# Eight modulation groups moved into the split weight stream, with the quarters of two projections between them

## The chip, the cores and the metric

The kernel runs on one core of a Trainium2 chip (trn2). TensorE (PE in the profile) does the matrix products, VectorE is DVE, ScalarE is ACT, GpSimd is POOL, and SyncE (SP) issues most of the transfers. The metric is the device time of one execution in microseconds; lower is better. The kernel before took 2410.05 us as the median of three runs (2409.24 to 2411.62).

## The reference, cut to what matters

Two transformer blocks work on 256 tokens of width 2048, all in float32. The change touches the start of the first block only: the modulation (a long vector times a 2048 x 12288 matrix, for two vectors `c` and `c_ctx`), the normalisation of `x` and `ctx`, and the first columns of the input projection.

```python
mod_l = (jax.nn.silu(c) @ w_ada[l] + b_ada[l])[:, None, :]
mod_c = (jax.nn.silu(c_ctx) @ w_ada[l] + b_ada[l])[None, None, :]
sh_a, sc_a, gt_a, sh_f, sc_f, gt_f = jnp.split(mod_l, 6, axis=-1)
csh_a, csc_a, cgt_a, csh_f, csc_f, cgt_f = jnp.split(mod_c, 6, axis=-1)
h_l = modulate(rms_norm(x, g_mix_norm[l]), sh_a, sc_a)      # h * (1 + scale) + shift
h_c = modulate(rms_norm(xc, g_mix_norm[l]), csh_a, csc_a)
qa_l, kva_l, kr_l, cb_l, cc_l, ch_l = split_projection(h_l @ w_in[l])
qa_c, kva_c, kr_c, cb_c, cc_c, ch_c = split_projection(h_c @ w_in[l])
```

Of the 24 groups of 512 columns of `w_ada`, groups 0 to 3 give the shift and 4 to 7 the scale that `h_l` and `h_c` need, so both vectors need groups 0 to 7; groups 8 to 23 are needed for `c` alone and later. The key-value columns of `w_in` (256 + 64) are applied to `h_l` and `h_c`, the query columns (512) to `h_l`.

## The kernel before, in words

**The weight stream.** All weights but `w_ada` come as chunks of 1 MB, 128 partitions x 2048 float32, in the order that `schedule()` (L63) writes down. SP loads chunk c into one of five buffers `raw` as soon as PE has finished chunk c-5 (L324 to L327). ACT copies a chunk into one of three buffers `hi`, rounded to fp32r (`split`, L379, L384), once PE has finished chunk c-3; DVE writes the remainder `lo` over `raw` (`split`, L921, L924). PE then makes three products for each pair of weight tile and activation tile: hi x hi, hi x lo, lo x hi (`three`, `chunk`). The activations have a hi and a lo part of the same kind (`act_hi`, `act_lo` for `x`, `u_hi`, `u_lo` for `ctx`). Every engine works through its own list in order and waits on semaphores.

**The modulation stream.** `w_ada` comes as 96 chunks of 1 MB of its own, four to a group, which POOL loads (L343). Groups 0 to 7 go through PE in plain float32, 2 columns (`silu_c` of both vectors) against 512 (`ada_rows`, L1900), into a row of PSUM; ACT copies the row out (L459) and PE turns it into columns (`ada_columns`, L1911). Four buffers serve here, two of which lie where `u_hi` and `u_lo` come later. Groups 8 to 23 are needed for one vector and are multiplied and summed on DVE, four instructions a chunk (`ada_chunk`, L931, L944), one chunk beside each chunk of the weight stream; PE only sums over the partitions (`ada_reduce`, L1855) and DVE adds the bias (`ada_take`).

**The order.** First come the modulation groups 0 to 7, with the normalisation of `x` and `ctx` beside them (L1088 to L1096). Then DVE applies scale and shift (`enter`, L1108) and makes the low halves in four quarters, and PE starts the key-value projection `kv_in` (4 chunks) and the query projection `q_in` (4 chunks). Modulation groups 8 and 9 run on DVE beside those two (`CARRY`, L313). Then comes a stretch of 46 chunks, counted by m: `conv_c0` (m 0 to 3), `kv_b` (4 and 5), `q_b` (6 to 9), `conv_in` (10 to 29) with the attention beside it, and `w_out` (30 to 45). At step m, ACT and DVE split the chunk m+2, and until m = 39 DVE takes one modulation chunk (L1301); PE reduces a group at m = 4, 8, ... 40 (L2040). Everything behind `w_out` is the same in both kernels.

## Time and profile before

| | |
|---|---|
| median of three runs | 2410.05 us |
| the profiled execution's own time | 2408.68 us |
| its span, first to last instruction | 2406.9 us |
| PE busy | 2319.2 us (96%), 17556 matmuls |
| DVE busy | 1505.5 us (63%) |
| ACT busy | 1008.8 us (42%) |
| moved by DMA | 471.85 MB, 196 GB/s on average |
| TensorE clock granted, mean | 0.986 of 2.4 GHz |

A busy PE is not a PE at its peak. The shares are means over the whole program; what one stage is worth is read from windows and from the chain of work that ended last. PEclk 1.00 stands for 2.4 GHz and 0.50 for 1.2 GHz.

### The profile page before, as it was taken

To read this page: it belongs to the slowest core of one execution; us is meant where nothing else is said; L and a number is where in the kernel's file an instruction comes from. 1 tells how busy PE (TensorE), PEld (TensorE's weight loads), DVE (VectorE), ACT (ScalarE), POOL (GpSimd) and SP (SyncE) were. 2 spreads that over 40 slices of the span, in tenths; PEclk is the share of its full clock that TensorE was granted. 3 is DMA by queue.
4 is the path that set the end of the run, shared out by engine and by line. 5 is a ranking of instruction groups with operands and counts; after the bars stand their busy time and mean duration, and the time that the engine had idled before them with its cause. 6 is when DMAs were issued, how large, how long until landed. Compare 5 with 4: busy or idle time off the path is not lost.

```text
span 2406.9 us, 39294 instructions
## 1 busy us (share of the span) xinstructions
PE 2319.2 (96%) x17556; PEld 2157.5 (90%) x17556; DVE 1505.5 (63%) x1703; ACT 1008.8 (42%) x965; POOL 59.0 (2%) x112
## 2 busy tenths in 40 slices
PE   6969989999999999999999899999999999999998
PEld 1249978898999999999999898989999999999998
DVE  2268787787888545555466758865567644445674
ACT  1023534433444334453344444445435435664352
POOL 1100000000000000000000000000000000000000
PEclk9989999999999999999999999999999999999999
DMA  9746765586676555555555454433544554334443
GB/s 394 277 146 258 295 232 212 213 309 247 243 265 246 201 181 182 186 178 190 177 190 191 155 181 158 154 112 138 178 174 160 190 182 156 118 140 175 168 162 126
DMA packets 64953, 471.85 MB, mean 196 GB/s; under 512 B 7216, under 2 KB 7216, under 8 KB 8336
## 3 DMA queue, kind: packets, MB, share of 16 engines
q1 hardware_dynamic: 50544, 365.65, 42.2%
q0 software_dynamic: 14096, 101.59, 11.2%
q8 instruction: 138, 2.26, 0.4%
q10 hardware_dynamic: 144, 2.10, 0.2%
q14 instruction: 31, 0.25, 0.0%
HBM read 467.21 MB, written 2.10 MB: 195 GB/s over the span
## 4 chain that ended last, share of the span: by engine, by line
PE 83%; DVE 10%; DMA 2%; ACT 2%; issue 2%; POOL 0%; DVEq 0%; ACTq 0%; POOLq 0%
PE acc L1780 72%; PE aux L1780 11%; DMA ada_raw<-ada_stream 2%; DVE lo L924 2%; ACT hi L384 1%; DVE ada_acc L944 1%; DVE x L1633 0%; DVE x L1630 0%; DVE rstd L1041 0%; DVE rstd L1057 0%; PE aux L1970 0%; DVE act_lo L1640 0%; ACT probs L727 0%; DVE rope_scratch L1479 0%; DVE rstd L1316 0%
## 5 line engine op out<-in xcount | busy, mean ns | idle before, releaser
L924 DVE TENSOR_TENSOR lo<-raw,hi 128x2048 fp32r<-128x2048 f32 x342 | 781.9, 2289 | 636.7 <-ACT hi L384 636.4
L384 ACT ACTIVATE hi<-raw 128x2048 fp32r<-128x2048 f32 x342 | 653.0, 1913 | 836.4 <-PE acc L1780 822.7
L1780 PE MATMUL acc<-act_hi,hi 128*128 128x256 f32 x4464 | 610.8, 289 | 36.5 <-DVE u_lo L1066 18.1
L1780 PEld LDWEIGHTS acc<-act_hi,hi 128*128 128x128 f32 x4464 | 570.6, 195 | 51.7 <-issue 40.4
L1780 PE MATMUL acc<-act_lo,hi 128*128 128x256 f32 x4464 | 591.8, 284 | 0.0
L1780 PE MATMUL acc<-act_hi,lo 128*128 128x256 f32 x4464 | 588.8, 283 | 0.0
L1780 PEld LDWEIGHTS acc<-act_lo,hi 128*128 128x128 f32 x4464 | 562.9, 193 | 0.0
L1780 PEld LDWEIGHTS acc<-act_hi,lo 128*128 128x128 f32 x4464 | 559.4, 192 | 0.0
L944 DVE SCALAR_TENSOR_TENSOR ada_acc<-ada_raw,silu_c,ada_acc 128x512 f32<-128x512 f32 x224 | 153.5, 743 | 6.8 <-DMA ada_raw<-ada_stream 6.2
L1780 PE MATMUL aux<-ada_raw,silu_c 128*2 128x512 f32 x256 | 113.6, 599 | 20.5 <-DMA ada_raw<-ada_stream 20.5
L1780 PEld LDWEIGHTS aux<-ada_raw,silu_c 128*2 128x2 f32 x256 | 20.8, 85 | 106.9 <-issue 94.1
L1780 PE MATMUL acc<-u_hi,hi 128*128 128x256 f32 x688 | 89.8, 283 | 0.0
L1780 PE MATMUL acc<-u_lo,hi 128*128 128x256 f32 x688 | 89.7, 283 | 0.0
L1780 PE MATMUL acc<-u_hi,lo 128*128 128x256 f32 x688 | 89.7, 283 | 0.0
L1780 PEld LDWEIGHTS acc<-u_lo,hi 128*128 128x128 f32 x688 | 85.7, 192 | 0.0
L1780 PEld LDWEIGHTS acc<-u_hi,lo 128*128 128x128 f32 x688 | 85.7, 192 | 0.0
L1780 PEld LDWEIGHTS acc<-u_hi,hi 128*128 128x128 f32 x688 | 85.7, 192 | 0.0
L636 ACT ACTIVATE y<-acc,vectors 128x256 f32<-128x256 f32 x86 | 41.7, 565 | 79.9 <-PE acc L1780 79.9
L343 POOL DMA_DIRECT2D ada_raw<-ada_stream x96 | 51.0, 532 | 701.8 <-DVE ada_acc L944 585.9
L1364 DVE SCALAR_TENSOR_TENSOR y<-acc,vectors,y 128x255 f32<-128x255 f32 x86 | 35.6, 475 | 49.3 <-ACT y L636 49.3
L727 ACT ACTIVATE probs<-probs,columns 128x256 f32<-128x256 f32 x32 | 16.0, 501 | 73.5 <-DVE columns L1568 73.5
L459 ACT ACTIVATE ada_acc<-aux 2x512 f32<-2x512 f32 x8 | 4.7, 585 | 98.9 <-PE aux L1780 98.9
(319 smaller groups left out, 1647.1 us busy)
## 6 DMA issues: line engine op xcount, KB each, us to landing
raw<-stream SPq DMA_DIRECT2D x342, 1024.0 KB, 4.8
ada_raw<-ada_stream POOLq DMA_DIRECT2D x96, 1024.0 KB, 5.4
x<-x_t SPq DMA_DIRECT2D x1, 2048.0 KB, 9.2
ctx<-ctx_t SPq DMA_DIRECT2D x1, 2048.0 KB, 16.1
x<-x_t ACTq DMA_DIRECT2D x1, 2048.0 KB, 8.9
out<-x SPq DMA_DIRECT2D x3, 512.0 KB, 7.5
p_raw<-p_t POOLq DMA_DIRECT2D x1, 512.0 KB, 4.8
out<-x SPq DMA_DIRECT2D x2, 256.0 KB, 2.0
```

Of the source, the lines that this page charges most:

```text
L343: eng.dma_start(ADA[slot][:, :], ada_stream[n]).then_inc(ada_full[slot], 16)
L384: nc.scalar.activation(HI[c % NH][:, :], RAW[c % NR][:, :], ACT.Copy).then_inc(hi_done, 1)
L459: nc.scalar.activation(FMA[ag % 2][0:2, 0, :], AUX[0:2, 1 + ag % 2, :], ACT.Copy)\
L636: nc.scalar.activation(Y[:, i, :], ACC[(base[0] + gi) % 2][:, t, :], ACT.Identity, scale=VV[:, bass.ds(w + 1, 1)], bias=VV[:, bass.ds(w + ...
L727: ins = nc.scalar.activation(s, s, ACT.Exp, bias=COL[:, 4 * (h % 2) + qt:4 * (h % 2) + qt + 1], accum_out=COL[:, 4 * (h % 2) + 2 + qt:4 * ...
L924: V.tensor_tensor(LO[c % NR][:, :], RAW[c % NR][:, :], HI[c % NH][:, :].bitcast(F32), ALU.subtract)\
L944: V.scalar_tensor_tensor(out=a, in0=w, scalar=s, in1=a, op0=ALU.mult, op1=ALU.add)\
L1364: ins = V.scalar_tensor_tensor(out=Y[:, i, 1:T], in0=acc[:, t, 0:T - 1], scalar=VV[:, bass.ds(w, 1)], in1=Y[:, i, 1:T], op0=ALU.mult, op1= ...
L1780: return TE.matmul(out, lhs, rhs, start=start, stop=stop, skip_group_check=True)
```

## The change

Groups 0 to 7 leave the modulation stream and enter the weight stream: each is four ordinary 1 MB chunks that ACT and DVE split into hi and lo. The stationary operand of PE is now four columns, the hi and lo part of both vectors (`C4`), and each of the four row blocks of a chunk takes one fp32r matmul with `hi` and one with `lo`, 8 a chunk. The 8 groups are ordered 0, 4, 1, 5, 2, 6, 3, 7, and one quarter of `kv_in` and of `q_in` (one chunk each) stands between them as soon as its quarter of shift and scale is known. Scale and shift are applied by ACT (`enter`), DVE keeps the low halves; the sums of squares are folded to four blocks by DVE additions and finished by PE (`tree`, `tree_total`) in place of a long DVE reduction. `x`, `consts` and `ctx` are loaded by the queue of ACT, ahead of its first work. Groups 8 and 9 move from beside `kv_in` and `q_in` into the stretch behind, so 48 modulation chunks stand in steps 4 to 41 by the list `ADA_STEPS` where 40 stood in steps 0 to 39; steps 4, 5, 10, 13, 15, 19, 21, 24, 29, 35 and 38 hold two. POOL loads the first two of them when PE has finished chunk 28.

```diff
+S0 = (("ada", 0), ("ada", 4), ("ada", 1), ("kv", 0), ("q", 0), ("ada", 5), ("ada", 2), ("kv", 1), ("q", 1), ("ada", 6),
+      ("ada", 3), ("ada", 7), ("kv", 2), ("q", 2), ("kv", 3), ("q", 3))
+ADA_ORDER = [i for kind, i in S0 if kind == "ada"]
+
+PLAN = [(kind, i, j) for kind, i in S0 for j in range(4 if kind == "ada" else 1)]
+ADA_END = [c for c, (kind, i, j) in enumerate(PLAN) if kind == "ada" and j == 3]
+
+ADA_STEPS = sorted([4, 4, 5, 5, 6, 7, 8, 9, 10, 10] + list(range(12, 42)) + [13, 15, 19, 21, 24, 29, 35, 38])
+BANK3_BUSY = (19, 21, 22, 23, 25, 26, 30, 31)
+REDUCE_AT, TAKE_AT = {}, {}
+for _g in range(12):
+    _m = ADA_STEPS[4 * _g + 3] + 1
+    while _m in BANK3_BUSY or _m in REDUCE_AT:
+        _m += 1
+    REDUCE_AT[_m] = 8 + _g
+    TAKE_AT[_m + 1] = 8 + _g
+
...
+    phases["kv_in"], phases["q_in"] = (0, 0), (0, 1)
+    for kind, i, j in PLAN:
+        if kind == "ada":
+            chunks.append(("w_ada", 0, list(range(4 * j, 4 * j + 4)), [(512 * i, 512 * i + 512)]))
+            continue
+        cols = [(Q_RANK, Q_RANK + KV_RANK), kr, kr] if kind == "kv" else [(0, Q_RANK)]
+        chunks.append(("w_in", 0, list(range(4 * i, 4 * i + 4)), cols))
+        if i == 3:
+            ENDS.append(("pe_chunk", len(chunks)))
+    groups[0] += 2
...
-            for n in range(4 * GTL):
-                if n >= 4:
-                    eng.wait_ge(ada_used, n - 3)
-                load(n, n % 4)
+            eng.wait_ge(pe_chunk, 28)
             for n in range(4 * GTL, 96):
-                if n < 4 * GTL + 2:
-                    eng.wait_ge(ada_used, n - 3)
-                else:
+                if n >= 4 * GTL + 2:
                     m = n - 2 - 4 * GTL
                     eng.wait_ge(ada_fma, 17 * (m // 4) + 4 * (m % 4 + 1))
                 load(n, n % 2)
...
-            def ada_row_copy(ag):
-                act.wait_ge(ada_used, 4 * ag + 4)
-                if ag >= 2:
-                    act.wait_ge(ada_sum, ag - 1)
-                nc.scalar.activation(FMA[ag % 2][0:2, 0, :], AUX[0:2, 1 + ag % 2, :], ACT.Copy)\
+            act.wait_ge(sem("silu_c"), 1)
+            nc.scalar.activation(C4[:, :, 0:2], SC[:, :].rearrange("p (v k) -> p k v", v=2), ACT.Copy)\
+                .then_inc(sem("silu_c"), 1)
+
+            def ada_row_copy(n):
+                act.wait_ge(pe_chunk, ADA_END[n] + 1)
...
-            def enter():
-                for q in range(4):
...
+            def enter(q, v):
+
+                a, dst, m, s0 = ((Y, AH, MOD, 0), (CTX, UH, MODC, KD))[v]
+                act.wait_ge(ada_out, 2 * q + 2)
+                act.wait_ge(sem("normalised"), v + 1)
+                for k in range(4 * q, 4 * q + 4):
+                    ins = nc.scalar.activation(a[:, k, :], a[:, k, :], ACT.Identity,
+                                               scale=SCL[:, s0 + k:s0 + k + 1], bias=m[:, k:k + 1])
+                ins.then_inc(step("nx_full")[0], 1)
+                hi_quarter(q, a, dst, "nx_full", "nx_hi", nth=2 * q + v + 1)
...
+            for p in range(len(PLAN)):
+                if p - 1 in ADA_END:
+                    ada_row_copy(ADA_END.index(p - 1))
+                split(p + 2)
+                if p == 2:
+                    act.wait_ge(sem("x_loaded"), 16)
+                    squares("nx", X, Y)
+                if p == 3:
+                    act.wait_ge(sem("ctx_loaded"), 16)
+                    squares("nc", CTX, SQC)
+                if p == 6:
+                    act.wait_ge(*since("nc_var", 1))
+                    nc.scalar.activation(RSTD[:, :], RSTD[:, :], ACT.Sqrt).then_inc(step("nc_std")[0], 2)
...
+            for p in range(len(PLAN)):
+                if p in [e + 2 for e in ADA_END[:7]]:
+                    rows_take(ADA_END.index(p - 2))
+                split(p + 2)
+                if p == 2:
+                    constants()
+                if p == 3:
+                    tree("nx", Y)
+                if p == 4:
+                    tree("nc", SQC)
+                if p == 6:
+                    in_variance("nx", 0)
+                    in_variance("nc", 1)
+                if p == 7:
+                    dve.wait_ge(*since("nc_std", 1))
+                    link(V.reciprocal(RSTD[:, :], RSTD[:, :]))
+                if p in (7, 8):
+                    normalise(p - 7)
+                if p in (10, 11):
+                    enter_low(0, p - 10)
...
+            def ada_rows(c, n, j):
+
+                pe.wait_ge(hi_done, c + 1)
+                if j == 0 and n >= 2:
+                    pe.wait_ge(ada_out, n - 1)
+                hi, lo = HI[c % NH], LO[c % NR]
+                for k in range(4):
+                    mm(AUX[0:4, 2 + n % 2, :], C4[:, 4 * j + k, :], hi[:, 512 * k:512 * k + 512], j == 0 and k == 0, False)
+                chunk_ready(c)
+                for k in range(4):
+                    ins = mm(AUX[0:4, 2 + n % 2, :], C4[:, 4 * j + k, :], lo[:, 512 * k:512 * k + 512], False,
+                             j == 3 and k == 3)
+                ins.then_inc(pe_chunk, 1)
...
+            n = -1
+            for c, (kind, i, j) in enumerate(PLAN):
+                if kind == "ada":
+                    n += j == 0
+                    ada_rows(c, n, j)
+                elif kind == "kv":
+                    if i == 2:
+                        ada_columns(7)
+                    kv_rows(c, i)
+                else:
+                    chunk(c, ACC[1], 4 * i, 4, i == 0, i == 3, AH, AL, lo_ready=(sem("in_ready"), i + 1))
+                if c - 1 in ADA_END[:7]:
+                    ada_columns(ADA_END.index(c - 1))
```

In the pieces of order below, `hi`, `lo` and `raw` are the buffers of the weight stream, `ada_raw` those of the modulation stream, `ada_acc` the sums of DVE, `aux` is PSUM, `silu_c` holds the two vectors. Shapes are partitions x elements of what is written.

PE at the program's start, before:

```order
L1780 MATMUL aux<-ada_raw_63,silu_c 2x512 [waits ada_full0,silu_c,ones]
L1780 MATMUL aux<-ada_raw_63,silu_c 2x512 x3
L1780 MATMUL aux<-ada_raw_64,silu_c 2x512 [waits ada_full1]
L1780 MATMUL aux<-ada_raw_64,silu_c 2x512 x3
L1780 MATMUL aux<-ada_raw_85,silu_c 2x512 [waits ada_full2]
L1780 MATMUL aux<-ada_raw_85,silu_c 2x512 x3
L1780 MATMUL aux<-ada_raw_86,silu_c 2x512 [waits ada_full3]
L1780 MATMUL aux<-ada_raw_86,silu_c 2x512 x3
```

and now, the start, then what follows chunk 4 (turning group 0 and the total for `x`), then the start of the first key-value quarter:

```order
L1861 MATMUL aux<-hi_59,silu_c_split 4x512 [waits silu_c,hi_done,ones]
L1861 MATMUL aux<-hi_59,silu_c_split 4x512 x3
L1861 MATMUL aux<-lo_54,silu_c_split 4x512 [waits lo_done]
L1861 MATMUL aux<-lo_54,silu_c_split 4x512 x3
...
L1861 MATMUL aux<-columns,ada_acc_65 128x2 [waits turn_selector,ada_row_out]
L1861 MATMUL aux<-columns,ada_acc_65 128x2 x3
L1861 MATMUL aux<-y,ones 128x256 [waits norm_ss]
L1861 MATMUL aux<-y,ones 128x256 x3
...
L1861 MATMUL acc<-act_hi,hi_59 128x256 [waits norm_hi,hi_done]
L1861 MATMUL acc<-act_hi,hi_59 128x256 x2
L1861 MATMUL aux<-u_hi,hi_59 128x256 x3
L1861 MATMUL acc<-act_hi,hi_59 128x256 x3
```

The long float32 products on `ada_raw` have become twice as many fp32r products on `hi` and `lo`, each with a wait on ACT or DVE that was not there, and the key-value quarter stands behind three groups instead of eight.

DVE from its start to the normalised `ctx`, before:

```order
L1089 TENSOR_REDUCE columns<-consts 128x1 [waits consts_loaded]
L1090 TENSOR_SCALAR consts<-consts,columns 128x256 [waits dve_chain]
L1041 TENSOR_REDUCE rstd<-y 128x256 [waits norm_sq,dve_chain]
L1054 TENSOR_SCALAR rstd<-aux 128x256 [waits norm_tot]
L1057 RECIPROCAL rstd<-rstd 128x256 [waits norm_std]
L1093 TENSOR_TENSOR y<-x,rstd 128x4096 [waits dve_chain]
L1041 TENSOR_REDUCE rstd<-ctx_squares 128x256 [waits norm_sq,dve_chain]
L1054 TENSOR_SCALAR rstd<-aux 128x256 [waits norm_tot]
L1057 RECIPROCAL rstd<-rstd 128x256 [waits norm_std]
L1096 TENSOR_TENSOR ctx<-ctx,rstd 128x4096 [waits dve_chain]
```

and now, from the split of chunk 7 to the taking of the second group:

```order
L962 TENSOR_TENSOR lo_56<-raw_51,hi_60 128x2048 [waits hi_done]
L962 TENSOR_TENSOR lo_57<-raw_52,hi_61 128x2048 [waits hi_done]
L1146 TENSOR_SCALAR rstd<-aux 128x256 [waits norm_tot] x2
L962 TENSOR_TENSOR lo_58<-raw_53,hi_59 128x2048 [waits hi_done]
L1328 RECIPROCAL rstd<-rstd 128x512 [waits norm_std]
L1151 TENSOR_TENSOR y<-x,rstd 128x4096 [waits dve_chain]
L962 TENSOR_TENSOR lo_54<-raw_49,hi_60 128x2048 [waits hi_done]
L1151 TENSOR_TENSOR ctx<-ctx,rstd 128x4096
L1160 TENSOR_TENSOR ada<-aux,vectors 128x4 [waits ada_sum]
L1161 TENSOR_TENSOR ada_ctx<-aux,vectors 128x4
L1166 SCALAR_TENSOR_TENSOR scales<-ada,vectors 128x4 [waits dve_chain]
L1166 SCALAR_TENSOR_TENSOR scales<-ada_ctx,vectors 128x4
```

The splits stand between the steps of the normalisation, in one list, and so does the taking of the modulation groups; the applying of scale and shift is no longer DVE's.

DVE late in `w_out`, steps 39 to 41, before (with the start of step 42):

```order
L924 TENSOR_TENSOR lo_58<-raw_53,hi_60 128x2048 [waits hi_done]
L944 SCALAR_TENSOR_TENSOR ada_acc_66<-ada_raw_64,silu_c,ada_acc_66 128x512 [waits ada_fma,ada_full1]
L944 SCALAR_TENSOR_TENSOR ada_acc_66<-ada_raw_64,silu_c,ada_acc_66 128x512 [waits ada_fma] x3
L948 TENSOR_TENSOR ada_acc_66<-ada_acc_66 128x512 [waits ada_fma]
L924 TENSOR_TENSOR lo_54<-raw_49,hi_61 128x2048 [waits hi_done]
L924 TENSOR_TENSOR lo_55<-raw_50,hi_59 128x2048 [waits hi_done]
L953 TENSOR_TENSOR ada<-aux,vectors 128x4 [waits ada_sum]
L924 TENSOR_TENSOR lo_56<-raw_51,hi_60 128x2048 [waits hi_done]
L1252 SCALAR_TENSOR_TENSOR x<-acc,ada,x 128x256 [waits pe_chunk,x_again]
```

and now, steps 39 to 41:

```order
L962 TENSOR_TENSOR lo_55<-raw_50,hi_59 128x2048 [waits hi_done]
L982 SCALAR_TENSOR_TENSOR ada_acc_66<-ada_raw_64,silu_c,ada_acc_66 128x512 [waits ada_fma,ada_full1]
L982 SCALAR_TENSOR_TENSOR ada_acc_66<-ada_raw_64,silu_c,ada_acc_66 128x512 [waits ada_fma] x3
L962 TENSOR_TENSOR lo_56<-raw_51,hi_60 128x2048 [waits hi_done]
L982 SCALAR_TENSOR_TENSOR ada_acc_66<-ada_raw_63,silu_c,ada_acc_66 128x512 [waits ada_fma,ada_full0]
L982 SCALAR_TENSOR_TENSOR ada_acc_66<-ada_raw_63,silu_c,ada_acc_66 128x512 [waits ada_fma] x3
L991 TENSOR_TENSOR ada<-aux,vectors 128x4 [waits ada_sum]
L962 TENSOR_TENSOR lo_57<-raw_52,hi_61 128x2048 [waits hi_done]
L982 SCALAR_TENSOR_TENSOR ada_acc_66<-ada_raw_64,silu_c,ada_acc_66 128x512 [waits ada_fma,ada_full1]
L982 SCALAR_TENSOR_TENSOR ada_acc_66<-ada_raw_64,silu_c,ada_acc_66 128x512 [waits ada_fma] x3
L986 TENSOR_TENSOR ada_acc_66<-ada_acc_66 128x512 [waits ada_fma]
L962 TENSOR_TENSOR lo_58<-raw_53,hi_59 128x2048 [waits hi_done]
```

Steps 40 and 41 had a split alone; each now has a modulation chunk, and the last sum is complete at step 41 instead of 39.

## Rows read from the trace of the kernel before

**Rows 1.** Windows: us, engine busy times (instructions), granted clock, DMA share, GB/s.
```profile
20.00:40.00 20.00, 15.29 (x36) 2.57 (x35) 7.73 (x3) 2.13 (x2) 2.28 (x5) 1.00 1.01 422
...
80.00:100.00 20.00, 20.00 (x59) 5.31 (x58) 0.00 (x0) 1.17 (x2) 2.65 (x5) 1.00 0.81 283
...
140.00:160.00 20.00, 3.16 (x20) 1.94 (x17) 16.56 (x34) 8.41 (x7) 1.15 (x2) 0.59 0.29 105
...
160.00:180.00 20.00, 18.71 (x145) 18.74 (x146) 20.00 (x30) 7.97 (x6) 0.53 (x1) 0.89 0.17 56
...
320.00:360.00 40.00, 40.00 (x280) 33.94 (x279) 29.21 (x46) 14.86 (x23) 2.12 (x4) 0.98 0.58 215
```

**Rows 2.** Chain that ended last, 140 to 260 us: start, length, what.
```profile
164.96 1.07 PE acc L1780 x9
...
198.15 5.86 PE acc L1780 x48
...
235.03 17.28 PE acc L1780 x144
```

**Rows 3.** Timeline of PE: start, length, instruction, idle before and its releaser.
```profile
14.11 8.66 PE L1780 MATMUL aux<-ada_raw,silu_c 128*2 128x512 f32 x16 [14.11 <-DMA ada_raw<-ada_stream]
...
28.34 3.60 PE L1780 MATMUL aux<-ada_raw,silu_c 128*2 128x512 f32 x8 [1.39 <-DMA ada_raw<-ada_stream]
...
161.29 0.55 PE L1780 MATMUL acc<-act_hi,hi 128*128 128x256 f32 x1 [18.13 <-DVE u_lo L1066]
```

**Rows 4.** Groups of instructions, 0 to 143 us: busy, mean ns, idle before.
```profile
L1041 DVE TENSOR_REDUCE rstd<-y 128x256 f32<-128x4096 f32 x1 | 7.1, 7091 | 0.0
...
L1093 DVE TENSOR_TENSOR y<-x,rstd 128x4096 f32<-128x4096 f32 x1 | 4.4, 4424 | 0.0
...
L441 ACT ACTIVATE y<-x 128x2048 f32<-128x2048 f32 x2 | 3.7, 1900 | 6.5 <-DMA x<-x_t 6.5
...
L446 ACT ACTIVATE rstd<-rstd 128x256 f32<-128x256 f32 x2 | 0.8, 416 | 14.7 <-DVE rstd L1054 14.7
...
L1780 PE MATMUL aux<-consts,ada_acc 2*128 2x2 f32 x64 | 8.2, 248 | 0.0
```

**Rows 5.** Costliest groups of the whole program: splits, modulation on DVE and PE.
```profile
L924 DVE TENSOR_TENSOR lo<-raw,hi 128x2048 fp32r<-128x2048 f32 x342 | 781.9, 2289 | 636.7 <-ACT hi L384 636.4
...
L384 ACT ACTIVATE hi<-raw 128x2048 fp32r<-128x2048 f32 x342 | 653.0, 1913 | 836.4 <-PE acc L1780 822.7
...
L944 DVE SCALAR_TENSOR_TENSOR ada_acc<-ada_raw,silu_c,ada_acc 128x512 f32<-128x512 f32 x224 | 153.5, 743 | 6.8 <-DMA ada_raw<-ada_stream 6.2
...
L1780 PE MATMUL aux<-ada_raw,silu_c 128*2 128x512 f32 x256 | 113.6, 599 | 20.5 <-DMA ada_raw<-ada_stream 20.5
```

**Rows 6.** DMA issues of the whole program, median us to landing.
```profile
ada_raw<-ada_stream POOLq DMA_DIRECT2D x96, 1024.0 KB, 5.4
...
x<-x_t SPq DMA_DIRECT2D x1, 2048.0 KB, 9.2
```

**Rows 7.** Window behind the restart of PE.
```profile
164.00:166.00 2.00, 2.00 (x18) 2.00 (x18) 2.00 (x3) 0.83 (x1) 0.00 (x0) 0.95 0.00 0
```

**Rows 8.** Timeline of DVE: the reciprocal of 512, and a modulation chunk that waits.
```profile
206.29 3.35 DVE L1057 RECIPROCAL rstd<-rstd 128x512 f32<-128x512 f32 x1 [0.70 <-ACT rstd L446]
...
298.24 2.74 DVE L944 SCALAR_TENSOR_TENSOR ada_acc<-ada_raw,silu_c,ada_acc 128x512 f32<-128x512 f32 x4 [2.70 <-DMA ada_raw<-ada_stream]
```

**Rows 9.** Timeline of PE: two waits behind `kv_in` and `q_in`.
```profile
313.07 2.08 PE L1780 MATMUL aux<-k_nope,q 128*128 128x512 f32 x2 [7.01 <-DVEq L1278]
...
538.02 1.05 PE L1780 MATMUL aux<-ones,ada_acc 128*128 128x1 f32 x8 [0.88 <-DVE ada_acc L948]
```

**Rows 10.** Timeline of DVE in `w_out`.
```profile
534.50 2.74 DVE L944 SCALAR_TENSOR_TENSOR ada_acc<-ada_raw,silu_c,ada_acc 128x512 f32<-128x512 f32 x4 [3.50 <-DMA ada_raw<-ada_stream]
```

**Rows 11.** Who waited for whom, 480 to 600 us: total, times, longest.
```profile
DVE lo L924 <- ACT hi L384: 12.9, 5, 4.3
```

**Rows 12.** DMA issues, 480 to 570 us.
```profile
ada_raw<-ada_stream POOLq DMA_DIRECT2D x12, 1024.0 KB, 7.4
```

289 lines of the change are left out of this document (141 added, 148 removed).

## The prediction

> **What bounds the kernel now.** I read the slices of the page first: PE is at 9 tenths nearly everywhere except in the first five of 40 slices (6, 9, 6, 9, 9), so the change can win only there. Then the windows of that start, the chain, and the timelines of PE and DVE.
>
> In 80 to 100 us PE is busy 20.00 of 20 us while ACT and DVE stand idle and DMA moves 283 GB/s of the 422 that it reached in 20 to 40 us [rows 1]. The 32 modulation chunks of groups 0 to 7 keep PE busy for 113.6 us, 3.55 each [rows 5]; early ones wait for their transfer besides (1.39 us) [rows 3]. They end at 143.2. Then comes a hole: PE waits 18.13 us for the first low quarter, until 161.29 [rows 3]; in 140 to 160 us it is busy 3.16 us, and DVE 16.56 [rows 1]. The projections behind are bound by PE, with DVE close: one fp32r matmul of 256 columns every 0.12 us (9 in 1.07; 48 in 5.86) [rows 2]. `conv_c0` ends and `kv_b` starts at 235.03 + 17.28 = 252.3 us [rows 2]. That is my yardstick: when does `kv_b` start now?
>
> **Supply and prices.** Forty chunks of 1.05 MB and 4.9 MB of inputs at 422 GB/s take 111 us, 2.5 us a chunk [rows 1]. A chunk costs DVE 2.29 us (2.2 from start to start), ACT 1.91 [rows 5]. For PE's price of 8 fp32r products of 512 columns I have no row with 4 columns of weights; twice the 0.12 us of 256 columns gives 1.9 us a chunk [rows 2], the bound above is the old 3.55. I take 1.9: it is the same number format and clock. All 32 are then 61 us; with the key-value quarters (72 x 0.12 = 8.65 us each), the query quarters (5.85), 8 turns of a group (8.2 in all, 1.03 each [rows 4]) and two folded totals (about 1.8) PE has 61 + 35 + 23 + 8 + 4 = 131 us. If all overlapped perfectly, PE would end the start at about 12 + 131 = 143. It does not, since the engines' lists are in order and only three `hi` buffers exist. I walk it.
>
> *To the first key-value quarter.* SP's chunk 0 shares DMA with `x` on ACT's queue. Before, `x` landed in 9.2 us [rows 6], and POOL's first 1 MB, beside it, let PE start at 14.11 [rows 3]; I put chunk 0 at 12.5 and chunk 4, when 10.2 MB are in, at 25. The Trainium skill (DMA: Bandwidth & Descriptors, section on queues and rings) says that each DMA engine takes turns between queues, a packet at a time; by equal turns chunk 0 would land at about 9 us, and the trace speaks against equal shares here. Chunk 4 is the same either way.
> From 27 us (its hi) DVE has: 10 low halves 22; folding, two of 2048 and two of 1024 elements, 6.8 (by the 2.29 of 2048) in place of two reductions of 7.09 [rows 4]; normalising 2 x 4.42 [rows 4]; reciprocal of 512, 3.4 [rows 8]; variances, takes, constants 2.9; two low quarters 2.3. Sum 46. Its waits: 3 for hi 5, behind the squares of `x` (3.7 [rows 4]); 3.8 for hi 9, behind the root, which waits for DVE itself; 3.6 for hi 12 and 13, behind ACT's `enter` (4 x 0.42 [rows 4], and a hi copy of half a chunk, 1.1 by the 1.91 [rows 5]: 2.8 each). So the low half of `ctx` is there at 27 + 46 + 10.4 = 83.5; the last two thirds of the key-value quarter follow, 5.8; q0 5.85; a turn 1.05; and 1.5 for a halved clock after a hole. PE is there at 98.
> *Eight groups' chunks, kv1, q1.* The first two chunks are split (2 x 1.9), six come at 2.5, the supply. Then enter(1) for `x` and `ctx` on ACT holds kv1's low products back to 125.5. Plus 5.8 + 1.05 + 5.85: 138.
> *Twelve chunks.* 2 x 1.9 + 10 x 2.5 = 29, plus 3 for enter(2) and 2 for POOL's two early loads, which share the DMA: 172. Row copy and turn of the last group, 2.
> *kv2, q2, kv3, q3.* 29 us; enter(3), 12 us from the same point, hides behind the first 14.5. The start ends at 203. Key-value total and its wait 2.7, `conv_c0` 23.4, query total 0.7: **`kv_b` at 229.8**, 22.5 us earlier. DVE turns the keys at m = 3, after both norms, which leaves one accumulator occupied 1.5 us longer: 21 us gained.
>
> **What is given back.** (1) Steps 4 to 10 carry 10 modulation chunks; six, not five, stand in steps 6 to 10, ahead of the query rotation, for which PE waits 7.01 us already [rows 9], in a stretch where DVE waits 2.70 us for a transfer [rows 8]. One chunk is 4 x 0.743 = 3.0 us, 2.7 start to start [rows 5]. I take 3.5; ends 0 and 6. (2) Two more reductions of a group stand in a stretch full of PE work: 2 x 1.0 us. (3) Steps 12 to 27 carry 21 chunks in place of 16, 14 us of DVE where it is busy 29.21 of 40 us [rows 1], so some 2.7 us idle in each of 16 steps: nothing. (4) Steps 28 to 41 carry 17 in place of 12: 13.7 us. Before, DVE has no idle worth naming there, but for 3.50 us at a transfer [rows 10], which made PE wait 0.88 us for a reduction [rows 9]; its other gaps there sum to 12.9 us, the longest 4.3 [rows 11], nearly all behind step 40. So 13.7 less what of these the late reductions at 36, 39 and 42 can use (some 8): PE loses 2 at step 36 and 4 at the end, 6 in all if transfers add 4. In these steps 17 + 14 MB go through in about 90 us, 360 GB/s, with two `ada_raw` buffers whose loads took 7.4 us [rows 12]. Ends 2 (the first wait alone) and 22 (all eight chunks of the stretch, 8 x 2.74, bare).
>
> **Sum**, against the execution's own 2408.7 us: 2408.7 - 21 + 3.5 + 2 + 6 = 2399.2. The median before was 2410.05, 1.4 more. I forecast **2399 us**.
>
> **Rivals.**
> *A. The start overlaps better.* For it: DVE's own work up to chunk 35 is 36 x 2.2 + 33 = 112 us, so from 12 us on it could be done at 124 and the start at 155 to 175, if the waits for hi behind `enter`, root and squares vanished. Against: each wait is an order in one list, read from code. With the start at 178 in place of 203: 2374.
> *B. Nothing left.* The gain of the start is smaller (210 in place of 203) and the reductions wait a little more (+3): 2409.
> *C. The modulation chunks moved into `w_out` decide.* One mechanism: in steps 28 to 41 DVE, without a gap before, gets 17 chunks, and each waits for one of two buffers. A buffer's round is the load, 7.4 as the median [rows 12], some 10 where two queues are full, + 2.7 of use: 5 to 6.5 us a chunk against 6.1 us of PE for a step with 1.2 chunks. At 6.5 the last nine chunks take 58 in place of 45 us and each reduction behind them holds PE. It decides from 15 us lost there; with 22, and only 15 won at the start, it is 2408.7 - 15 + 5.5 + 22 = 2421. For it: the 3.50 and 0.88 us. Against: it happened once in 12 chunks.
> *D. The clock.* Around PE's hole the granted clock was 0.59 in 140 to 160 us [rows 1], and 0.95 in 164 to 166, three us after the restart [rows 7]. In the new start PE has holes of 3 to 6 us between chunks up to the first key-value quarter. With PE at 0.76 of its time in short gaps the clock stayed at 1.00 [rows 1]; I charged 1.5 us. Were it 0.50 (1.2 GHz) through all modulation chunks, each would cost 3.8 us, more than the supply's 2.5: 20 chunks behind the first quarter x 1.3 = 26 us more, and 2425. The Trainium skill (TensorE: Matmul & The Clock Gate, section on HAM oscillation) says that idling between bursts of products throttles PE again and again; by that rule it is D. The trace has both cases, and the gaps of 0.6 us expected in the later chunks are nearer to the one that kept 1.00.
>
> **Chances.** Forecast (2392 to 2405) 0.45, A 0.15, B 0.20, C 0.13, D 0.07. Less than 0.2% (4.8 us, about what a measurement of this kernel can tell from no change) counts as the same. Faster: 0.45 + 0.15 + a part of B, 0.62; same 0.18; slower C, D, 0.20. The range leaves out the ends of A and of C and D: 2376 to 2418.
>
> **What would show it.** In the profile after: first PE work at about 14 to 17 us; the first `act_hi` product at about 81 and `conv_c0` from about 205; `kv_b` at 230. Modulation chunks on PE at 0.22 to 0.24 us a product, granted clock 1.00 from 100 us on. DVE busy 75% or more of 30 to 170 us, waiting for hi. The wait for the rotated queries 9 to 12 us in place of 7.01. Waits of PE for `ada_acc` at steps 36, 39 and 42, 2 to 8 us in all. From `up0` on the same durations. Wrong would be: a modulation chunk at 3.4 us or more, the start before 185 or after 215, or over 15 us lost in `w_out`.

## The result and the profile after

| | median of the runs | lowest to highest | profiled execution, its span |
|---|---|---|---|
| before (20 runs) | 2408.99 us | 2407.07 to 2411.62 | 2408.68, 2406.9 |
| after (20 runs) | 2413.12 us | 2406.10 to 2420.82 | 2419.05, 2417.3 |

The ratio is 1.0022, with a 95% interval of 1.0016 to 1.0028: 4 us slower, where 10 us faster were forecast. The changed kernel's executions also spread over 14.7 us, the old one's over 4.6, and its profiled one lies 5.9 us above their median. A second profiled execution of the same kernel (the run `again` below) took 2413.07 us, so I read both.

The windows that answer [rows 1] in the changed kernel (columns as there):

```profile
20.00:40.00 20.00, 11.14 (x36) 3.73 (x37) 14.58 (x10) 17.66 (x11) 0.00 (x0) 0.73 0.96 401
80.00:100.00 20.00, 18.58 (x130) 18.22 (x131) 9.83 (x8) 7.23 (x6) 0.00 (x0) 0.82 0.23 84
140.00:160.00 20.00, 17.50 (x84) 7.16 (x82) 13.32 (x10) 13.51 (x11) 1.20 (x2) 1.00 0.85 337
160.00:180.00 20.00, 15.38 (x49) 5.68 (x49) 15.35 (x11) 17.10 (x16) 0.00 (x0) 0.66 0.94 376
320.00:360.00 40.00, 40.00 (x286) 33.94 (x285) 37.77 (x61) 15.93 (x25) 3.17 (x6) 1.00 0.73 279
```

The hole of 140 to 160 us is gone (PE busy 17.50 us instead of 3.16). But PE now has gaps in each of the windows before 180 us, and the granted clock fell to 0.66 in 160 to 180. DVE went from 29.21 to 37.77 us of the 40 in 320 to 360 us, with PE busy throughout. From the first to the last scores DVE was busy 121.2 of 149 us, against 110.4 of 150 before.

PE's timeline of the changed kernel, the rows that decide (start, length, instruction, idle before it and its releaser):

```profile
14.84 1.44 PE L1861 MATMUL aux<-hi,silu_c_split 128*4 128x512 f32 x3 [14.84 <-ACT hi L399]
```

```profile
81.42 0.98 PE L1861 MATMUL acc<-act_hi,hi 128*128 128x256 f32 x3 [4.07 <-ACT u_hi L444]
```

```profile
123.65 0.98 PE L1861 MATMUL acc<-act_hi,hi 128*128 128x256 f32 x3 [4.85 <-ACT u_hi L444]
```

```profile
226.38 0.70 PE L1861 MATMUL aux<-rstd,ones 128*128 128x256 f32 x2 [2.06 <-DVE rstd L1079]
226.73 3.48 PE L1861 MATMUL acc<-act_hi,hi 128*128 128x256 f32 x16
```

```profile
288.81 1.84 PE L1861 MATMUL aux<-ones,ada_acc 128*128 128x1 f32 x8 [2.51 <-issue]
290.51 3.76 PE L1861 MATMUL acc<-act_hi,hi 128*128 128x256 f32 x16
...
306.32 2.08 PE L1861 MATMUL aux<-k_nope,q 128*128 128x512 f32 x2 [7.60 <-DVEq L1359]
...
310.33 2.07 PE L1861 MATMUL acc<-act_hi,hi 128*128 128x256 f32 x8
```

```profile
484.94 2.08 PE L1861 MATMUL acc<-act_hi,lo 128*128 128x256 f32 x16
491.43 3.58 PE L1861 MATMUL aux<-mix_squares,selector 128*4 128x256 f32 x8 [4.42 <-DVE ada L991]
494.94 3.07 PE L1861 MATMUL acc<-act_hi,hi 128*128 128x256 f32 x16
```

```profile
582.39 1.84 PE L1861 MATMUL aux<-ones,ada_acc 128*128 128x1 f32 x8 [2.65 <-issue]
584.09 3.76 PE L1861 MATMUL acc<-act_hi,hi 128*128 128x256 f32 x16
```

The first modulation product comes at 14.84 us, against 14.11 of before [rows 3]. The first key-value quarter begins at 81.42 us, after 4.07 us of waiting, the second after 4.85. The query rotation is waited for 7.60 us, against 7.01 [rows 9]. In `w_out` PE waits 4.42 us for `ada`, the column sums of modulation group 15, which before it never did. The 8 and the 16 products behind it then take 3.58 and 3.07 us, where before they took 1.89 and 2.17: the granted clock was 0.57 in 491 to 498 us. Behind the wait at 582.39, 16 products took 3.76 us at 0.50, that is 1.2 GHz.

VectorE's timeline of the changed kernel, with the waits for transfers and the place of the 4.42 us:

```profile
285.24 2.74 DVE L982 SCALAR_TENSOR_TENSOR ada_acc<-ada_raw,silu_c,ada_acc 128x512 f32<-128x512 f32 x4 [2.53 <-DMA ada_raw<-ada_stream]
...
296.41 2.08 DVE L982 SCALAR_TENSOR_TENSOR ada_acc<-ada_raw,silu_c,ada_acc 128x512 f32<-128x512 f32 x3 [3.38 <-DMA ada_raw<-ada_stream]
```

```profile
488.57 2.73 DVE L982 SCALAR_TENSOR_TENSOR ada_acc<-ada_raw,silu_c,ada_acc 128x512 f32<-128x512 f32 x4
491.22 0.15 DVE L991 TENSOR_TENSOR ada<-aux,vectors 128x4 f32<-128x4 f32 x1
```

```profile
537.90 0.88 DVE L979 TENSOR_SCALAR ada_acc<-ada_raw,silu_c 128x512 f32<-128x512 f32 x2 [2.62 <-DMA ada_raw<-ada_stream]
...
556.28 2.74 DVE L982 SCALAR_TENSOR_TENSOR ada_acc<-ada_raw,silu_c,ada_acc 128x512 f32<-128x512 f32 x4 [2.02 <-DMA ada_raw<-ada_stream]
...
569.05 2.74 DVE L982 SCALAR_TENSOR_TENSOR ada_acc<-ada_raw,silu_c,ada_acc 128x512 f32<-128x512 f32 x4 [3.42 <-DMA ada_raw<-ada_stream]
```

Where before had 2.70 us at one transfer ahead of the query rotation [rows 8] and 3.50 us in `w_out` [rows 10], there are now 2.53 + 3.38 and 2.62 + 2.02 + 3.42. The page's groups of the whole program, against [rows 5]:

```profile
L962 DVE TENSOR_TENSOR lo<-raw,hi 128x2048 fp32r<-128x2048 f32 x374 | 855.0, 2290 | 669.7 <-ACT hi L399 669.3
L399 ACT ACTIVATE hi<-raw 128x2048 fp32r<-128x2048 f32 x374 | 713.8, 1912 | 882.6 <-PE acc L1861 828.2
...
L982 DVE SCALAR_TENSOR_TENSOR ada_acc<-ada_raw,silu_c,ada_acc 128x512 f32<-128x512 f32 x224 | 153.1, 745 | 13.3 <-DMA ada_raw<-ada_stream 12.7
...
L1861 PE MATMUL aux<-hi,silu_c_split 128*4 128x512 f32 x128 | 42.7, 463 | 19.4 <-ACT hi L399 19.4
L1861 PE MATMUL aux<-lo,silu_c_split 128*4 128x512 f32 x128 | 41.5, 454 | 14.4 <-DVE lo L962 14.2
```

A split costs what it did (2290 and 1912 ns), on 32 chunks more. The modulation products on PE are new: all 32 chunks kept PE busy for 42.7 + 41.5 = 84.2 us, 2.6 a chunk. The 1.9 that I had charged is what a chunk took from start to start at full clock (1.86): four products took 1.09 us at full clock and 1.87 where it was halved, as in about half of those ahead of the first quarter (granted clock 0.72 on average in 14 to 81 us). DVE's waits for `ada_raw` rose from 6.2 to 12.7 us. DMA issues of 480 to 570 us, against [rows 12]:

```profile
ada_raw<-ada_stream POOLq DMA_DIRECT2D x13, 1024.0 KB, 7.5
```

**Lead over before at five marks**, in us (positive is earlier). The marks are starts in the timelines: the first `acc<-kv_hi,hi` product (`kv_b`), the first and the last `aux<-k_nope,q` product (scores, steps 11 and 26), the `rstd<-y` reduction of DVE at the end of `w_out`, and the last stretch of 672 products in the chain. Before: 252.13, 313.07, 462.88, 586.20, 2319.80 us.

| run | kv_b | first scores | last scores | end of w_out | last stretch | median, us |
|---|---|---|---|---|---|---|
| forecast | 22.5 | 17.5 | 15.5 | 9.5 | 9.5 | 2399 |
| after | 12.22 | 6.75 | 7.53 | -10.42 | -10.35 | 2413.1 |
| again | 12.28 | 6.92 | 7.56 | -4.10 | -4.39 | 2413.1 (one) |
| before, 8 and 9 moved | 5.67 | 0.23 | -0.05 | -12.16 | -13.96 | 2420.8 |
| without 8, 9; 10 to 19 from step 0 | 11.90 | 2.48 | 2.06 | 1.73 | 1.53 | 2405.1 |
| without 8, 9; rest unmoved | 12.54 | 17.42 | 16.84 | 3.72 | 3.46 | 2405.2 |
| 8, 9 in the start | -2.06 | -1.92 | -2.29 | -2.95 | -1.27 | 2409.5 |
| small loads | 13.37 | 13.54 | 13.20 | 7.92 | 11.68 | 2401.6 |
| small products | 11.69 | 10.75 | 11.08 | 7.32 | 9.44 | 2397.4 |
| quarters later | 18.02 | 11.90 | 11.98 | -0.48 | -0.69 | 2406.1 |
| pair at 26 | 14.77 | 8.85 | 8.18 | 1.95 | 4.12 | 2410.8 |
| pairs at 25 to 27 | 12.04 | 5.81 | 4.57 | -5.78 | -3.75 | 2412.3 |
| query total at 2 | 14.97 | 2.54 | 2.65 | -8.96 | -6.74 | 2415.4 |
| four early | 8.55 | 5.52 | 5.03 | -4.32 | -4.28 | 2408.3 |
| more in attention | 15.38 | 14.60 | 13.83 | 3.76 | 5.91 | 2404.3 |
| its pair at 28 | 11.59 | 12.11 | 10.78 | 0.38 | 2.33 | 2405.6 |
| **more in attention, quarters later** | 19.86 | 20.20 | 18.98 | 8.66 | 10.68 | **2397.5** |

Leads are of one execution each, medians of 5 to 20. Some of these executions lie well off their kernel's median: 6.2 us under it in "pair at 26", 4.6 under in "small loads", 3.2 over in "quarters later" and 4.7 in "four early". Two of the same kernel agree within 0.2 us up to the last scores and differ by 6.3 in `w_out`; the nine executions with the changed kernel's own start had leads of 11.6 to 15.4 at `kv_b`. So differences of 3 us in one column of two rows say little.

### The profile page after: what moved, and what is told of

Read it like the earlier page. It is cut to its first block, busy times and chain, and to the rows that moved or that the text cites. A ratio compares the mean times of both kernels' runs of the same rounds, so it can differ in the third digit from the quotient of the medians.

```text
span 2417.3 us, 39444 instructions
## 1 busy us (share of the span) xinstructions
PE 2303.3 (95%) x17568; PEld 2175.8 (90%) x17568; DVE 1562.1 (65%) x1724; ACT 1083.3 (45%) x1029; POOL 41.9 (2%) x80
## 4 chain that ended last, share of the span: by engine, by line
PE 81%; DVE 9%; ACT 4%; DMA 3%; issue 2%; SPq 0%; DVEq 0%; ACTq 0%
PE acc L1861 72%; PE aux L1861 9%; DVE lo L962 2%; ACT hi L399 2%; DMA raw<-stream 2%; DMA ada_raw<-ada_stream 1%; DVE ada_acc L982 1%; DVE x L1714 0%; DVE x L1711 0%; DVE rstd L1095 0%; DVE act_lo L1721 0%; PE aux L2070 0%; ACT ctx L485 0%; ACT probs L765 0%; DVE rope_scratch L1560 0%
## 5 line engine op out<-in xcount | busy, mean ns | idle before, releaser
L962 DVE TENSOR_TENSOR lo<-raw,hi 128x2048 fp32r<-128x2048 f32 x374 | 855.0, 2290 | 669.7 <-ACT hi L399 669.3
L399 ACT ACTIVATE hi<-raw 128x2048 fp32r<-128x2048 f32 x374 | 713.8, 1912 | 882.6 <-PE acc L1861 828.2
L982 DVE SCALAR_TENSOR_TENSOR ada_acc<-ada_raw,silu_c,ada_acc 128x512 f32<-128x512 f32 x224 | 153.1, 745 | 13.3 <-DMA ada_raw<-ada_stream 12.7
L1861 PE MATMUL aux<-hi,silu_c_split 128*4 128x512 f32 x128 | 42.7, 463 | 19.4 <-ACT hi L399 19.4
L1861 PE MATMUL aux<-lo,silu_c_split 128*4 128x512 f32 x128 | 41.5, 454 | 14.4 <-DVE lo L962 14.2
L1861 PEld LDWEIGHTS aux<-hi,silu_c_split 128*4 128x4 f32 x128 | 11.5, 94 | 41.7 <-issue 24.0
L1861 PEld LDWEIGHTS aux<-lo,silu_c_split 128*4 128x4 f32 x128 | 10.7, 92 | 42.3 <-DVE lo L962 25.0
```

Source lines behind the costliest of these rows:

```text
L399: nc.scalar.activation(HI[c % NH][:, :], RAW[c % NR][:, :], ACT.Copy).then_inc(hi_done, 1)
L962: V.tensor_tensor(LO[c % NR][:, :], RAW[c % NR][:, :], HI[c % NH][:, :].bitcast(F32), ALU.subtract)\
L982: V.scalar_tensor_tensor(out=a, in0=w, scalar=s, in1=a, op0=ALU.mult, op1=ALU.add)\
L1861: return TE.matmul(out, lhs, rhs, start=start, stop=stop, skip_group_check=True)
```

## Experiments

First the halves of the change and versions that leave out a part of the computation, then the order of the start and single waits, then other spreads of the chunks. Pieces of code are cut; `...` stands for what is left out.

**The changed kernel again.** No edit.

> The changed kernel once more, word for word, for a second profiled execution: its executions lay between 2406.1 and 2420.8 us, and the profiled one, at 2419.05, 5.9 above the median. If the waits of the w_out stretch are what varies, the lead at step 27 (458.5 us in the first profile) is the same within 1 us, and the end of w_out is not.

Measured: 2413.07 us. PE's timeline of this run:

```profile
306.15 2.08 PE L1861 MATMUL aux<-k_nope,q 128*128 128x512 f32 x2 [7.26 <-DVEq L1359]
```

```profile
491.42 3.58 PE L1861 MATMUL aux<-mix_squares,selector 128*4 128x256 f32 x8 [4.43 <-DVE ada L991]
```

```profile
547.87 3.45 PE L1861 MATMUL acc<-act_hi,hi 128*128 128x256 f32 x16 [2.08 <-DVE x L1301]
```

The rotation's wait and the 4.4 us are there again, to 0.2 us. The waits of 0.88 and 2.65 us at the reductions behind steps 39 and 42 are not: the second half of `w_out` is what varies. What differed between the two executions there I did not find; DVE waited 8.6 us for transfers in 480 to 600 us in the first and 4.5 in the second.

**One half of the change alone.** In the kernel before, groups 8 and 9 moved as the change does:

```
-    CARRY = {"kv_in": (8, 4), "q_in": (9, 4), "up0": (20, 2)}
+    CARRY = {"up0": (20, 2)}
...
-                if m < 40:
-                    ag = 10 + m // 4
...
+                for i in [i for i, at_step in enumerate(ADA_STEPS) if at_step == m]:
+                    ag, j = GTL + i // 4, i % 4
```

> The kernel before with its own start, and only modulation groups 8 and 9 taken out of the two input projections and put into the steps of conv and w_out as the changed kernel does (48 chunks in steps 4 to 41, the same reductions). Theory W: the projections gain 1 to 3 us, the steps behind lose 13 to 18, so 2419 to 2425 us. Rival S (the moved chunks are nearly free, the loss is by the new start): 2408 to 2412 us.

Measured: 2420.75 us, ratio 1.0055 (1.0039 to 1.0071). `kv_b` came 5.67 us earlier, the scores not at all, and `w_out` gave 12.1 back. Its wait before the squares is that of the changed kernel:

```profile
499.02 3.56 PE L1791 MATMUL aux<-mix_squares,selector 128*4 128x256 f32 x8 [4.42 <-DVE ada L964]
```

So the move of 8 chunks costs 11.7 us without any new start, and 17.4 from `kv_b` on. The 5.7 us won ahead of it are mostly the hole of PE before the projections, 13.34 us instead of 18.13. The start of the change is worth the rest: 12.22 - 5.67 = 6.6 us at `kv_b`, 2420.8 - 2413.1 = 7.6 at the end.

**The other half, with groups 8 and 9 left out.** First with the 40 remaining chunks one a step from step 0, as in the kernel before, then at the changed kernel's own places.

```
-ADA_STEPS = sorted([4, 4, 5, 5, 6, 7, 8, 9, 10, 10] + list(range(12, 42)) + [13, 15, 19, 21, 24, 29, 35, 38])
+ADA_STEPS = list(range(40))                                                    # first
+ADA_STEPS = sorted([10, 10] + list(range(12, 42)) + [13, 15, 19, 21, 24, 29, 35, 38])   # second
```

> The changed kernel with modulation groups 8 and 9 left out altogether (8 chunks of 1 MB: their loads, their products and their two reductions; the columns hold the bias alone), and groups 10 to 19 one chunk a step as in the kernel before. It shows what the new start is worth with nothing moved behind it. Theory W (the start leaves 12.4 us of lead at the key-value up-projection, what is lost later is lost by the moved chunks): 2394 to 2400 us. Rival S (the new start leaves a state, by clock or by the common stream, that costs in attention and w_out whatever the chunks do): 2405 to 2412 us.

> The changed kernel with modulation groups 8 and 9 left out (8 chunks, their columns hold the bias alone), and the 40 others at exactly the changed kernel's own steps, so that steps 4 to 9 carry none. The step of the query rotation (first attention scores) began at 306.3 us in the changed kernel with 7.6 us of wait, and at 310.6 us where groups 10 to 12 stood in steps 0 to 10. Theory Q (from the key-value up-projection to the first scores the modulation chunks, each waiting 8 to 10 us for its load, set VectorE's time and not TensorE's arrival): the scores begin at 292 to 297 us and the wait is under 3 us; the w_out stretch, with its 17 chunks unchanged, still gives back 8 to 18 us, so 2398 to 2405 us. Rival R (the wait is the weight stream's or the rotation's own): scores at 303 to 306 us, 2408 to 2413 us.

Measured: 2405.14 us (0.9982, 0.9974 to 0.9991) and 2405.21 us (0.9987, 0.9977 to 0.9997). The first missed the expectation of theory W by 5 us and landed in the range of rival S, but not where S had its loss: it lost 9.4 us between `kv_b` and the scores, 0.4 in the attention steps and 0.3 in `w_out`. Chunks at steps 0 to 3 stand ahead of the key-value norm on DVE, PE waited 6.94 us inside `kv_b`, and the scores came only 2.5 us earlier. In `w_out` it has 12 chunks and four reductions, as the kernel before. The second shows both prices apart. PE's timeline:

```profile
295.65 2.08 PE L1863 MATMUL aux<-k_nope,q 128*128 128x512 f32 x2 [4.77 <-DVEq L1361]
```

```profile
482.13 3.21 PE L1863 MATMUL aux<-mix_squares,selector 128*4 128x256 f32 x8 [4.43 <-DVE ada L992]
```

With no chunk in steps 4 to 9 the scores begin at 295.65 us, 10.7 earlier than in the changed kernel, as theory Q had it, though the wait stays at 4.77, where Q had under 3. And `w_out`, 17 chunks unchanged, takes 13.1 us of the lead again. Of the 9.3 us by which this version led the second execution of the changed kernel at the last scores, 7.8 are left at the end of `w_out`, and 7.9 in the medians: what was won earlier is kept, and `w_out` takes its price all the same.

**Groups 8 and 9 inside the start.**

```
-ADA_STEPS = sorted([4, 4, 5, 5, 6, 7, 8, 9, 10, 10] + list(range(12, 42)) + [13, 15, 19, 21, 24, 29, 35, 38])
+ADA_STEPS = [0] * 8 + sorted(list(range(4, 11)) + list(range(12, 40)) + [13, 15, 19, 21, 24])
+START_STEPS = [12, 14, 16, 18, 22, 24, 26, 28]
...
-            eng.wait_ge(pe_chunk, 28)
+            eng.wait_ge(pe_chunk, 8)
...
+                for i in [i for i, at_step in enumerate(START_STEPS) if at_step == p]:
+                    ag, j = GTL + i // 4, i % 4
+                    ada_chunk(ag, j, EARLY[ag - GTL], (ag - GTL) * 17 + 4 * j, j % 2, ...
```

> The changed kernel with the whole computation, but groups 8 and 9 multiplied by VectorE inside the start (one chunk behind the splits of plan places 12, 14, 16, 18, 22, 24, 26, 28, into two accumulators of their own, reduced at steps 0 and 1), and groups 10 to 19 one chunk a step from 4 to 39 (none at 11), with second ones at 13, 15, 19, 21 and 24: in w_out 12 chunks, reduced behind 32, 36 and 40 as in the kernel before. Theory W (moving the 8 chunks behind the start is what costs; VectorE has 40% of the start free): kv_b begins 0 to 5 us later than in the changed kernel, the w_out stretch loses under 3 us against before, 2396 to 2403 us. Rival D (loads and VectorE are as full in the start, each of the 8 chunks holds the splits up for 2.7 us): kv_b begins 15 to 20 us later, 2408 to 2416 us.

Measured: 2409.47 us (1.0002, 0.9993 to 1.0011). Rival D by the start (14 us later than the changed kernel), theory W by `w_out` (0.7 us lost with 12 chunks). The 8 chunks, with their loads from chunk 8 on, cost 14 us there; only the old start, whose projections waited anyway, took them for 5.7.

**Loads or products.**

```
-                eng.dma_start(ADA[slot][:, :], ada_stream[n]).then_inc(ada_full[slot], 16)
+                w = 256 if 34 <= n < 80 else CHUNK
+                eng.dma_start(ADA[slot][:, 0:w], ada_stream[n][:, 0:w]).then_inc(ada_full[slot], 16)
```
and, in the other,
```
+                wide = 64 if n0 < 204 and n0 not in (0, 17) else 512
...
+                    w = ADA[slot][:, 512 * k:512 * k + wide]
```

> The changed kernel with 46 of the 48 modulation chunks of steps 4 to 41 (all but the first two) loaded only in their first 256 of 2048 columns, an eighth of the bytes; VectorE multiplies all 2048 as before (the rest of a buffer is what an earlier chunk left). Theory M (the loads of the modulation chunks set the pace: 8 to 10 us each before the scores, waits of 2 to 3.4 us in w_out): the scores begin at 294 to 299 us instead of 306, the w_out stretch loses under 5 us, 2396 to 2402 us. Rival V (VectorE's own 2.75 us a chunk and the order on it decide): scores at 302 to 306 us, the w_out stretch loses 8 to 12 us, 2409 to 2413 us.

> The changed kernel with the same 48 chunks loaded whole, but VectorE's products of them cut to 64 of 512 columns an operation (apart from the first chunk of groups 8 and 9, and the later columns of the accumulators keep what they had). Theory V (VectorE's work on the chunks decides, above all in w_out, where it was 81% busy over 480 to 600 us): the wait before the first w_out squares is gone, the w_out stretch loses under 3 us, 2396 to 2403 us. Rival M (the loads decide): the waits for `ada_raw` stay, 2408 to 2413 us.

Measured: 2401.62 us (0.9965, 0.9953 to 0.9978) and 2397.43 us (0.9957, 0.9944 to 0.9971). Neither theory alone. Between `kv_b` and the scores the changed kernel lost 5.4 us; with small loads nothing is lost there, with small products 0.9. In `w_out` they lose 5.3 and 3.8 us instead of 11.7 to 17.9; the wait ahead of the squares is 4.42 us still with small loads and 1.25 with small products, so it is DVE's work and order and not the loads. The other waits of PE behind it are gone in both. PE's timeline of the first and of the second:

```profile
485.77 3.47 PE L1862 MATMUL aux<-mix_squares,selector 128*4 128x256 f32 x8 [4.42 <-DVE ada L992]
```

```profile
484.72 1.89 PE L1862 MATMUL aux<-mix_squares,selector 128*4 128x256 f32 x8 [1.25 <-DVE ada L992]
```

Groups of DVE in 480 to 600 us of the second:

```profile
L983 DVE SCALAR_TENSOR_TENSOR ada_acc<-ada_raw,silu_c,ada_acc 128x64 f32<-128x64 f32 x50 | 10.9, 277 | 11.0 <-DMA ada_raw<-ada_stream 11.0
...
L980 DVE TENSOR_SCALAR ada_acc<-ada_raw,silu_c 128x64 f32<-128x64 f32 x6 | 1.2, 251 | 7.1 <-DMA ada_raw<-ada_stream 7.1
```

With products of 277 instead of 743 ns DVE waits 18.1 us for transfers instead of 8.6: they had been hidden behind its work. By the code a chunk's load and its work follow one another in a buffer, which would be why shortening either one helps; that is argued, the runs show only that both do.

**The order of the start.** Each key-value and query quarter one modulation group later:

```
-S0 = (("ada", 0), ("ada", 4), ("ada", 1), ("kv", 0), ("q", 0), ("ada", 5), ("ada", 2), ("kv", 1), ("q", 1), ("ada", 6),
-      ("ada", 3), ...
+S0 = (("ada", 0), ("ada", 4), ("ada", 1), ("ada", 5), ("kv", 0), ("q", 0), ("ada", 2), ("ada", 6), ("kv", 1), ("q", 1),
+      ("ada", 3), ...
```

> The changed kernel with only the order of the start altered: the first key-value and query quarters stand behind four modulation groups (0, 4, 1, 5) and not three, the second behind six (then 2, 6) and not five, so that the quarters' inputs are ready when TensorE comes to them (it waited 4.07 us at 81.4 and 4.85 us at 123.7 us, and ran the products behind each at half the clock). Theory S (the start fell 9 to 10 us short of its forecast by those waits and the clock behind them): kv_b begins 4 to 8 us earlier, at 232 to 236 us. As the 17 chunks of w_out stay, most of that is given back there: 2408 to 2412 us. Rival B (the loads bound the start, 375 GB/s at 142 to 180 us): kv_b within 2 us of 240, 2412 to 2415 us.

Measured: 2406.12 us (0.9986, 0.9975 to 0.9996), 7 less than the changed kernel. PE's timeline, the first products of the two quarters (93 and 131 us), without a wait, and the one wait of `w_out` that is not in the row of the squares:

```profile
93.29 0.51 PE L1861 MATMUL acc<-act_hi,hi 128*128 128x256 f32 x3
```

```profile
131.58 0.51 PE L1861 MATMUL acc<-act_hi,hi 128*128 128x256 f32 x3
```

```profile
544.00 3.78 PE L1861 MATMUL acc<-act_hi,hi 128*128 128x256 f32 x16 [5.33 <-DVE x L1301]
```

`kv_b` came 5.8 us earlier, as theory S had it. Against the nine executions with the old order (mean lead 12.9) the two with this one (18.0 and 19.9) are 6 us earlier. The gain was also kept to the end, against my expectation: 7.0 us in the medians. `w_out` took 12.5 us all the same.

**Single waits.** One doubled chunk from step 29 to 26; all three of `w_out` to 25, 26, 27; the query total and norm one step later:

```
-... + [13, 15, 19, 21, 24, 29, 35, 38])
+... + [13, 15, 19, 21, 24, 26, 35, 38])                            # first
+... + [13, 15, 19, 21, 24, 25, 26, 27])                            # second
...
-                if m == 1:                                                       # third
+                if m == 2:
                     totals("nq", T)
```

> The changed kernel (2413.1 us in the median) with one doubled modulation chunk moved from step 29 to step 26, so that group 15 is complete at 27, reduced behind step 28 and taken at 29, as in the kernel before, and not reduced behind 29 and taken at 30. Theory W (TensorE's wait of 4.42 us before the first w_out squares, at 487 to 491 us, with the 1.7 us of halved clock behind it, is a wait of its own): 2407 to 2409 us, the wait for `ada_out` there is gone. Rival L (VectorE has too much to do in steps 28 to 41, one wait is like another): the wait comes back at a later reduction, 2412 to 2414 us.

> The changed kernel with all three doubled modulation chunks of the w_out stretch (29, 35, 38) moved to steps 25, 26 and 27: 14 chunks instead of 17 in steps 28 to 41. Theory W (the modulation chunks of the w_out stretch decide, and the attention steps before it have room): the lead at step 27 stays near 7 us, the w_out stretch gives back about 8 instead of 18 us, 2402 to 2407 us. Rival L (VectorE and the two raw buffers are as full in the attention steps): 2411 to 2415 us, with TensorE's waits now before step 28.

> The changed kernel with the query total (TensorE waited 2.06 us for it and then ran its next 16 products at half the clock) and the query normalisation one step later, so that neither is on the path to the key-value up-projection. The products of the up-projection begin at 243.05 us in the changed kernel. Theory Q (what comes earlier there is waited away before the scores): they begin 2 to 3.5 us earlier, the scores begin within 1.5 us of 306, and the time stays within 2 us of 2413. Rival P (TensorE's time is the path there): all of it reaches the end, 2409 to 2411 us.

Measured: 2410.82 us (1.0006, 0.9997 to 1.0015), 2412.34 (1.0013, 1.0004 to 1.0021) and 2415.40 (1.0027, 1.0018 to 1.0035). The first removed the 4.42 us and 2.3 us of the time, less than the 4 to 6 expected; PE then waited 2.94 us at 541.84 us for an accumulator that DVE's gated addition frees (1.47 and 2.08 us in the two executions of the changed kernel). The second put a wait of 4.87 us at the reduction behind step 28, after three doubled steps in a row: as rival L. The third was 2.7 us earlier at `kv_b`, within what executions of the same start differ by, and 4.2 later than the changed kernel at the scores (PE waited 4.82 us for ACT inside `kv_b` and 9.12 for the rotation). Its interval overlaps the changed kernel's (1.0016 to 1.0028): it won nothing, and that it is slower isn't shown.

**Versions with all of the computation.** 7 chunks in steps 4 to 10, 27 in 12 to 27, 14 in 28 to 41; then with the last pair at 28; with group 8 at the end of the start (and 7, 23 and 14 behind); and the first once more with the start's order above.

```
+ADA_STEPS = sorted(list(range(4, 11)) + list(range(12, 42)) + [12, 13, 14, 15, 17, 18, 19, 21, 25, 26, 27])
```

> The changed kernel with the 48 chunks spread otherwise: one a step at 4 to 10 (7 instead of 10), 27 instead of 21 in the attention steps 12 to 27, 14 instead of 17 in 28 to 41; all is computed. If the attention steps have room, the scores begin near 301 us, the lead over before at step 27 is near 10 us and w_out gives back 5: 2402 to 2406 us. Rival (they are full, their chunks make TensorE wait there): 2409 to 2415 us.

> The spread that gave 2404.3 us with its last doubled chunk at step 28 instead of 27, so that three doubled steps do not stand right ahead of the reduction behind step 28, for which TensorE waited 4.87 us and ran 2.3 us longer behind it at half the clock. If that wait is of its own: 2400 to 2403 us. If it comes back at the reductions of w_out: 2403 to 2407 us.

> The changed kernel with group 8's four chunks multiplied at plan places 36 to 39, that is while TensorE does the last four key-value and query quarters (180 to 209 us, in which the load queues stood still for about 10 us), into an accumulator of its own, reduced behind step 0; then 7 chunks in steps 4 to 10, 23 in 12 to 27, 14 in 28 to 41; all is computed. If VectorE has room at 180 to 209 us: kv_b as in the changed kernel within 2 us, scores near 300 us, 2400 to 2405 us. Rival (the four chunks hold the key-value chain up): kv_b 6 to 11 us later, 2408 to 2412 us.

> The same order of the start together with the spread of the 48 chunks that gave 2404.3 us (7 in steps 4 to 10, 27 in 12 to 27, 14 in 28 to 41). Theory S: kv_b begins 4 to 8 us earlier than there (236.8 us in its profile), and with fewer chunks in w_out more than half of it is kept: 2399 to 2402 us. Rival B: within 1.5 us of 2404.

Measured: 2404.28 us (0.9982, 0.9974 to 0.9991), 2405.55 (0.9984, 0.9975 to 0.9993), 2408.29 (1.0000, 0.9992 to 1.0009) and **2397.46 us (0.9953, 0.9940 to 0.9965)**, which beats both kernels: 11.3 us under before, 15.7 under the change. It also lies 1.5 us under its expected range. The two measures add up: the order alone won 7.0 us, the spread alone 8.8, both 15.7. The windows of 320 to 460 us in the changed kernel and in the first of these:

```profile
320.00:460.00 140.00, 140.00 (x961) 114.78 (x960) 118.21 (x182) 59.31 (x87) 10.03 (x19) 1.00 0.66 251
```

```profile
320.00:460.00 140.00, 140.00 (x972) 115.99 (x972) 122.77 (x190) 58.86 (x87) 11.66 (x22) 1.00 0.73 278
```

These are the same times and not the same steps, since the second kernel runs 6 to 8 us ahead. From its own first to its last scores DVE was busy 132.3 of 150.5 us, against 121.2 of 149 in the changed kernel and 110.4 of 150 before, and PE was busy in all of it: the attention steps had the room. PE's timeline of the last version:

```profile
292.87 2.07 PE L1861 MATMUL aux<-k_nope,q 128*128 128x512 f32 x2 [7.64 <-DVEq L1359]
```

```profile
468.45 1.84 PE L1861 MATMUL aux<-ones,ada_acc 128*128 128x1 f32 x8 [4.87 <-DVE ada L991]
470.15 3.76 PE L1861 MATMUL acc<-act_hi,hi 128*128 128x256 f32 x16
```

The wait of 4.87 us and 3.4 us of lower clock behind it are still there; the pair at 28 only made it 6.17. With one of 1.08 us just ahead it is PE's only wait from step 27 to the end of `w_out`, so that it makes most of the 10.3 us lost there, and not the number of chunks: three doubled steps in a row stand ahead of two reductions behind steps 27 and 28 that take turns in one PSUM bank. The second of these waits for the sums of the first, which DVE takes behind a chunk. With the pair at 26 alone, where steps 25 and 27 hold one chunk, the same wait was 0.68 us. The four early chunks failed because a product of 2.75 us stands ahead of the key-value total there (PE waited 5.57 us for it instead of 2.19).

## Why the prediction was wrong

*The start, 21 us gained.* This step failed. The lead at `kv_b` was 12.2 us, not 22.5. The walk was right in its order, and fell behind step by step: the first two quarters ended at 99.8 us (98 forecast), the second two at 141.6 (138), the twelve chunks at 178.6 (172), the last quarters at 209.4 (203), and `kv_b` began 27.6 us behind `conv_c0`'s first product (24.1). That is 1.8, 3.6, 6.6, 6.4 and 10.1 us late. I had charged 1.5 us for a halved clock, once. PE ran at 1.2 GHz behind the holes at 81 and 123 us, in 163 to 176 (granted clock 0.50) and at 226 us. Putting the quarters where their inputs are ready won 5.8 us at `kv_b`; that is shown. That need not be the same 5.8 us that the forecast missed, since the walk had counted a part of these waits. How the missing 10 us divide is read from the trace alone. Up to the end of the twelve chunks it is 6.6 us, with the waits and the clock at the two quarters, the halved clock of 163 to 176 us, and transfers at 376 GB/s in 160 to 180. Between the end of the start and `kv_b` it is 3.7 more: PE waited 2.06 us for the query total, which the walk did not have, and lost 1.7 to the clock behind it. The run with that total one step later took the wait away and got others for it, and no run tells the rest apart.

*(1) and the keys, 5 us before the scores.* Right: 5.4 us in both profiles. The rotation's wait grew only to 7.60 us and not to 9 to 12, because the reduction behind step 10 had already held PE for 2.51 us (row 288.81), with 3.1 of clock behind it. The version with the pairs at 25 to 27, the same up to there, had no wait at the reduction and one of 13.08 us at the rotation, and began the scores within 1 us of the changed kernel. I had priced DVE's work alone; the loads are as much of it: small loads win all of the 5.4 us back, small products 4.5.

*(2), (3), reductions, and nothing in steps 12 to 27.* (3) is right: the lead grew by 0.7 us there with DVE's share up as said, and the versions with 25 chunks up to step 26, in place of 20, lost 0.8 to 1.3. The 2 us of (2) did not show there because they stand elsewhere: up to step 26 both kernels have six reductions, and from 27 on the changed one has six (27, 29, 32, 36, 39, 42) for four (28, 32, 36, 40). They belong to `w_out`, at 0.8 us each.

*(4) `w_out`, 6 us.* The place was right and the size too small: 11.7 us in one execution, 17.9 in the other. I had counted DVE's idle time and given transfers 4 us. What I missed is a wait by order: group 15, complete at step 28, is reduced behind step 29 and its sums are taken in step 30 behind another chunk (DVE rows 488.57, 491.22), while PE's squares behind step 30 need the same PSUM bank. That is 4.42 us and 2.6 of clock behind it. The run with the pair at 26, which reduces group 15 behind step 28, had no such wait. The second that I missed is the accumulator that DVE's gated addition frees: 2.08 us in the second execution and 1.5 of clock. With two more reductions and less the 0.88 us of before, these sum to 11.4 of that execution's 11.7 us. At steps 36, 39 and 42, where I looked, PE waited 0, 0.88 and 2.65 us in the first execution, within the 2 to 8 forecast, and 0 in the second. Rival C had the place and the two buffers, at 22 us.

*Sum.* By the execution at the median: -12.3 + 5.4 - 0.6 + 11.7 = +4.2 us, and 0.3 behind `w_out`; forecast was -22.5 + 5 + 2 + 6 = -9.5. Of the 14 us missed, 10.2 are the start and 5.7 `w_out`, less 2.6 in the attention steps, of which 1.6 are the two reductions that I had put there. Rival A is refuted: the start ended at 209.4, not 178. B had that end (210) and too little behind it; what came is B's start with half of C's loss. D did not come: from 100 us to the start's end, the clock was halved in 123 to 128 and 163 to 176 us alone, and ahead of the first quarter, where it was halved about half of the time, PE waited for its inputs anyway.

## What to carry to other kernels

Work moved off a start that waits must be priced where it lands: the same 8 chunks cost 5.7 us in the old projections, 14 in the new start and 17 behind it. Five more chunks in steps where PE was busy without a gap and DVE had a fifth of its time free cost 1.4 to 2.1. Do not price such work by its amount alone. In `w_out` 17 chunks of full size cost 11.6 to 17.9 us, 16 cost 6.2 in one execution, 14 or 15 cost 9.4 to 10.4 and 12 cost 0.3 to 0.7, and the waits behind these numbers are of order: a reduction whose sums are taken late, while the next product needs the same bank or the same accumulator. A lead that was won earlier mostly came through here, and two independent gains added up. Place a product behind the point at which its inputs are ready, even if that means later: the quarters moved back by one group won 7 us.

## What the runs showed of the hardware beyond that

A hole on PE can cost more than its length. Behind most waits of 2.5 to 6 us, the first 16 products took 3.1 to 3.8 us instead of 2.1 and the next 16 often 2.3 to 3.1, so 1 to 3.4 us more. The length of the wait does not settle it: behind the same 2.19 us at the key-value total the 16 took 2.47 us in most runs and 3.99 in "small loads" and "pair at 26". Late in the program, in code that the change leaves alone, all kernels have the same wait of 1.78 us. Behind it the kernel before lost 1.6 us to the clock and the last version nothing: that much of its lead in the last column is luck. PE's timeline of before, then of the last version:

```profile
2246.24 2.01 PE L1780 MATMUL aux<-rstd,ones 128*128 128x256 f32 x4 [1.78 <-DVE rstd L1627]
2247.69 3.19 PE L1780 MATMUL acc<-act_hi,hi 128*128 128x256 f32 x16
```

```profile
2237.15 1.13 PE L1861 MATMUL aux<-rstd,ones 128*128 128x256 f32 x4 [1.77 <-DVE rstd L1708]
2237.93 2.26 PE L1861 MATMUL acc<-act_hi,hi 128*128 128x256 f32 x16
```

A lower clock also came without a hole right ahead. PE's timeline of the changed kernel:

```profile
511.46 1.99 PE L1861 MATMUL aux<-rstd,consts 4*128 4x256 f32 x8
513.38 1.30 PE L1861 MATMUL aux<-ones,ada_acc 128*128 128x1 f32 x8
514.54 3.43 PE L1861 MATMUL acc<-act_hi,hi 128*128 128x256 f32 x16
```

In the kernel before, behind the same short products, the same 16 took 2.16 us (at 513.86).

The time was less steady where PE waited for the accumulator of the gated addition (`DVE x L1301`, 1.47 to 5.33 us). The six versions that have this wait, all with doubled chunks of full size at steps 35 and 38, spread over 11.6 to 14.7 us from the lowest to the highest; the kernel before and the nine versions without it over 2.1 to 8.8. That this wait is what varies is read from the match and not shown. Why it comes longer in one execution than in the next stays open.
